# One decoder step on one core: the attention's work in another order, and the last stage shared out over four engines

## The reference, cut to what matters

```python
q = (xn @ wq).reshape(B, T, MEM_HEADS, MEM_HEAD_DIM)
s = jnp.einsum('bthd,bmhd->bhtm', q, k).astype(jnp.float32) * (MEM_HEAD_DIM ** -0.5)
p = jax.nn.softmax(s, axis=-1)
o = jnp.einsum('bhtm,bmhd->bthd', p, v).reshape(B, T, D_MODEL)
x = x + o @ wo
...
logits = (xt @ router_w).astype(jnp.float32)
top_v, top_i = lax.top_k(logits, TOP_K)
gates = jax.nn.softmax(top_v, axis=-1)
for e in range(N_EXPERTS):
    out = out + combine[:, e:e + 1] * swiglu(xt, wg[e], wu[e], wd[e])
...
return rmsnorm(x, P['final_norm'])
```

## Time and profile before

| what | value |
|---|---|
| median of 3 runs | 1127.97 us (1124.49 to 1130.51) |
| the profiled execution, whole | 1124.33 us |
| its span | 1122.5 us |
| PE busy | 1060.7 us (94%) |
| DVE busy, ACT busy, POOL busy | 781.1 us, 653.8 us, 21.4 us |
| shares of the chain that ended last | PE 74%, DVE 13%, ACT 6%, DMA 4% |

### The profile page before, as it was taken

One profiled execution on the slowest core, in us unless ns is written; L12 is line 12 of the kernel. 1 busy time (PEld: TensorE's weight loads), 2 busy tenths in 40 slices (PEclk: granted clock), 3 DMA queues, 4 the chain that ended last, 5 costly groups with the idle time before them and its releaser, 6 DMA issues.

```text
span 1122.5 us, 19890 instructions
## 1 busy us (share of the span) xinstructions
PE 1060.7 (94%) x7693; PEld 1003.4 (89%) x7693; DVE 781.1 (70%) x1080; ACT 653.8 (58%) x900; POOL 21.4 (2%) x40
## 2 busy tenths in 40 slices
PE   4999899999999998998999979999999999999994
PEld 4999897799999998998987869899999999999983
DVE  5597653575655556588553559798889888888973
ACT  5667433554433444576543457777767767776761
POOL 0001000000000000001010000000000000000000
PEclk8999999999999999999999989999999999999998
DMA  9454469946555555444469728898989898898951
GB/s 373 160 178 144 145 218 355 378 153 207 174 185 187 179 178 162 151 151 144 154 227 363 271 86 339 296 365 290 363 293 361 291 342 311 329 324 312 346 204 41
DMA packets 64275, 272.99 MB, mean 243 GB/s; under 512 B 7328, under 2 KB 7584, under 8 KB 63552
## 3 DMA queue, kind: packets, MB, share of 16 engines
q1 hardware_dynamic: 62352, 264.33, 66.1%
q0 software_dynamic: 1408, 7.12, 1.7%
q10 hardware_dynamic: 432, 0.38, 0.1%
HBM read 265.83 MB, written 5.98 MB: 242 GB/s over the span
## 4 chain that ended last, share of the span: by engine, by line
PE 74%; DVE 13%; ACT 6%; DMA 4%; issue 2%; SPq 1%; DVEq 0%; ACTq 0%
PE bank L645 11%; PE bank L648 11%; PE bank L650 11%; PE bank L649 11%; PE bank L646 11%; PE bank L647 11%; DMA ring<-dense 4%; DVE wl L1488 3%; ACT wh L1088 2%; DVE rstd L1482 2%; DVE sq L1499 1%; PE bank L672 1%; PE bank L765 1%; PE bank L937 1%; PE bank L938 1%
## 5 line engine op out<-in xcount | busy, mean ns | idle before, releaser
L1488 DVE TENSOR_TENSOR wl<-ring,wh 128x1024 fp32r<-128x1024 f32 x170 | 206.8, 1224 | 183.9 <-ACT wh L1088 182.4
L645 PE MATMUL bank<-xh,wh 128*128 128x264 f32 x928 | 271.2, 292 | 20.1 <-DVE xl L1504 17.1
L1088 ACT ACTIVATE wh<-ring 128x1024 fp32r<-128x1024 f32 x170 | 178.9, 1056 | 158.5 <-PE bank L647 121.3
L1757 DVE TENSOR_TENSOR wl<-ring,wh 128x1408 fp32r<-128x1408 f32 x144 | 232.5, 1623 | 52.8 <-ACT wh L1349 52.6
L646 PE MATMUL bank<-xl,wh 128*128 128x264 f32 x928 | 266.8, 288 | 0.0
L647 PE MATMUL bank<-xh,wl 128*128 128x264 f32 x928 | 266.3, 287 | 0.0
L1349 ACT ACTIVATE wh<-ring 128x1408 fp32r<-128x1408 f32 x141 | 194.7, 1381 | 52.5 <-PE bank L650 51.0
L645 PEld LDWEIGHTS bank<-xh,wh 128*128 128x128 f32 x928 | 178.1, 192 | 28.1 <-issue 23.0
L649 PE MATMUL bank<-wh,xl 128*128 128x352 f32 (+4 forms) x560 | 185.5, 331 | 0.0
L646 PEld LDWEIGHTS bank<-xl,wh 128*128 128x128 f32 x928 | 178.5, 192 | 0.0
L647 PEld LDWEIGHTS bank<-xh,wl 128*128 128x128 f32 x928 | 177.9, 192 | 0.0
(11 more groups left out here) (256 smaller groups left out, 1722.1 us busy)
## 6 DMA issues: line engine op xcount, KB each, us to landing
ring<-experts SPq DMA_DIRECT2D x192, 704.0 KB, 6.0
ring<-dense SPq DMA_DIRECT2D x234, 512.0 KB, 3.8
o_k<-kv POOLq DMA_DIRECT2D x2, 1024.0 KB, 4.3
o_v<-kv POOLq DMA_DIRECT2D x2, 1024.0 KB, 7.4
x<-xT SPq DMA_DIRECT2D x2, 528.0 KB, 5.0
o_y<-sq SPq DMA_DIRECT2D x4, 264.0 KB, 2.1
gatew<-gate_w POOLq DMA_DIRECT2D x2, 512.0 KB, 8.2
mem<-memT SPq DMA_DIRECT2D x1, 1024.0 KB, 13.4
```

What stands on the lines that cost most here:

```text
L645: mm(out, s_hi, m_hi, start=start, stop=False)
L1088: A(parts(k)[0], raw(u), ACT.Copy).then_inc(hi_ready, 1)
L1488: V.tensor_tensor(w_lo, raw(u), w_hi.bitcast(F32), ALU.subtract)\
L1757: V.tensor_tensor(w_lo, eraw(jj % ESLOTS), w_hi.bitcast(F32), ALU.subtract)\
```

## The change

**Attention.** PE takes the samples' scores of the last head directly behind those of the third, ahead of the prompt's scores; the samples' probabilities are turned between the two halves of the prompt's scores; the samples' values are spread between other work instead of standing in pairs. DVE and ACT treat the samples' softmax first. Both splitters run one unit less ahead in the queries (`4` for `5`). DVE copies the samples' result (`o8`) ahead of the first low part of `mo`, not behind it. POOL's stores of keys and values wait until the first bank of `mo` is full.

**Experts.** PE's wait for the rounded identity moves from ahead of the first gather to the place where the identity is used. PE, ACT and DVE load the count earlier: ACT and DVE ahead of the pass, PE in its last pair.

**The end.** The body that runs without `extra` is now the branch's first arm. PE scatters the first four chunks as soon as the first half of the last expert's result is split, and sums squares between later chunks. ACT squares each chunk when DVE has added it, multiplies `x` by `final_norm` itself, and has the square root's table loaded early. The last multiplication is split: DVE makes chunks 0, 1, 2, 4, 6 and POOL 3, 5, 7.

The number of ring slots is 10 before and after, although the change's title names it.

```diff
-                                if hp + hh + t + c == 1 and hp == 1:
+                                if hp + hh + t + c == 0:
                                     frees(i, ("kc", l, 15))
...
+                sample_scores(NH - 1)
                 prompt_scores(0)
-                sample_scores(NH - 1)
-                prompt_scores(1)
...
-                pe.wait_ge(p_ready, 5 * l + 3)
+                pe.wait_ge(p_ready, 5 * l + 1)
...
+                prompt_scores(1)
                 for h in (0, 1):
                     prompt_probs(h)
                 pe.wait_ge(pz_ready, l + 1)
                 sample_values(0)
-                sample_values(1)
                 for h in (2, 3):
                     prompt_probs(h)
+                sample_values(1)
...
                 for m in range(KC):
                     prompt_values(m)
-                sample_values(2)
+                    if m == 4:
+                        sample_values(2)
                 sample_values(3)
...
+                pe.wait_ge(ident_ready, 1)
                 for side in range(2):
...
+            def finish(ps):
+
+                num, before = ps.after, block_of(ps.last, "b")
+
+                def square_sum(m):
+                    b = take_bank(ps.final_sum) if m == 0 else bank(ps.final_sum)
+                    pe.wait_ge(fsq_ready, m + 1)
+                    i = mm(b[:, 0:T], ones[:, :], sq[:, m, :], start=(m == 0), stop=(m == KC - 1))
+                    if m == KC - 1:
+                        full(i, ps.final_sum)
+
+                wait_read(pe, *before("D0"))
+                for c in range(4):
+                    scatter_chunk(c, num)
+                wait_read(pe, *before("D1"))
+                for c in range(4, KC):
+                    scatter_chunk(c, num)
+                    square_sum(c - 4)
+                for m in range(4, KC):
+                    square_sum(m)
...
+                elif p == main.p0 + main.np - 1:
+                    fetch_count()
...
-            pe.wait_ge(ident_ready, 1)
...
+            with pe.If(counted[0] <= CAP):
+                finish(main)
+            with pe.Else():
+                scatter(main.after, block_of(main.last, "b"))
                 run_pass(extra)
-            with pe.Else():
-                pe.nop()
...
-                        S.upto(behind("mq", l, m, 5, start("mo", l)))
+                        S.upto(behind("mq", l, m, 4, start("mo", l)))
...
+                    if last and u == 0:
+                        A(small[:, 95:96], eps[:, 0:1], ACT.Sqrt)
...
+            def finish(ps):
+                for m in range(KC):
+                    wait_read(act, *ps.after(f"C{m}"))
+                    A(sq[:, m, :], x[:, m, :], ACT.Square).then_inc(fsq_ready, 1)
+
+                def final_gain(m):
+                    k = VEC_FINAL + m
+                    act.wait_ge(fsq_ready, m + 1)
+                    A(x[:, m, :], x[:, m, :], ACT.Copy, scale=vec[:, k:k + 1]).then_inc(xf_ready, 1)
+
+                for m in range(4):
+                    final_gain(m)
+                wait_full(act, ps.final_sum)
+                A(rms[:, 0, :], bank(ps.final_sum)[:, 0:T], ACT.Sqrt, bias=eps[:, 0:1], scale=1.0 / D).then_inc(frms_ready, 1)
+                for m in range(4, KC):
+                    final_gain(m)
+
             act.wait_ge(route_ready, 1)
             count = act.value_load(need[0:1, 0:1], min_val=0, max_val=T)
+            run_pass(main)
...
-                S.upto(start("mo", l) + 1, 0)
                 n = tiles[("pvs", l)]
                 wait_full(dve, n)
                 read(V.tensor_copy(o8, bank(n)[:, 0:HD]), n)
+                S.upto(start("mo", l) + 1, 0)
...
+            def finish():
+
+                dve.wait_ge(frms_ready, 1)
+                V.reciprocal(rstd[:, 0, :], rms[:, 0, :]).then_inc(frstd_ready, 1)
+                dve.wait_ge(frstd_ready, 1)
+                for m in (0, 1, 2, 4, 6):
+                    dve.wait_ge(xf_ready, m + 1)
+                    V.tensor_tensor(xn[:, m, :], x[:, m, :], rstd[:, 0, :], ALU.mult).then_inc(y_ready, 1)
...
+                wait_full(pool, tiles[("mo", l, 0)])
                 pool.dma_start(o_k[l], kT).then_inc(kv_written, 16)
...
+            pool.wait_ge(frstd_ready, 1)
+            for m in (3, 5, 7):
+                pool.wait_ge(xf_ready, m + 1)
+                G.tensor_tensor(xn[:, m, :], x[:, m, :], rstd[:, 0, :], ALU.mult).then_inc(y_pool_ready, 1)
```

More of the change, by code:

```diff
@@ L155, in bank_plan @@
         out += [("scs", l)]
-        out += [("sc", l, t, hp) for hp in range(2) for t in range(2)]
+        out += [("sc", l, t, 0) for t in range(2)]
         out += [("pts", l)]
+        out += [("sc", l, t, 1) for t in range(2)]
         out += [("pt", l, h) for h in range(NH)]
@@ L207, in __init__ @@
             self.end = self.tail + len(TAIL)
+            self.final_sum = self.end
         def first(self, kind):
@@ L1042, in run_pass @@
                 pair(p1, ps.last, ps.earlier(p1), last=True)
-                scatter(ps.after, block_of(ps.last, "b"))
             for t in range(3):
@@ L1047, in _, with fetch_count @@
                     wait_read(pe, tiles[("tk", l, t, hp)])
-            pe.wait_ge(ident_ready, 1)
+            counted = []
+            def fetch_count():
+                pe.wait_ge(route_ready, 1)
+                counted.append(pe.value_load(need[0:1, 0:1], min_val=0, max_val=T))
             run_pass(main)
-            pe.wait_ge(route_ready, 1)
-            count = pe.value_load(need[0:1, 0:1], min_val=0, max_val=T)
-            with pe.If(count > CAP):
+            with pe.If(counted[0] <= CAP):
+                finish(main)
+            with pe.Else():
+                scatter(main.after, block_of(main.last, "b"))
                 run_pass(extra)
-            with pe.Else():
-                pe.nop()
-            for m in range(KC):
-                pe.wait_ge(fsq_ready, m + 1)
-                i = mm(psum[0][:, 0:T], ones[:, :], sq[:, m, :], start=(m == 0), stop=(m == KC - 1))
-            i.then_inc(fsum_ready, 1)
+                finish(extra)
         @block.scalar
@@ L1239, in _ @@
                     if m % 2:
-                        S.upto(behind("mq", l, m, 5, start("mo", l)))
+                        S.upto(behind("mq", l, m, 4, start("mo", l)))
+                n = tiles[("scs", l)]
+                act.wait_ge(max_ready, 5 * l + 1)
+                read(A(prs, bank(n)[:, 0:NM], ACT.Exp, bias=nmx[:, 8:9], scale=HD ** -0.5, accum_out=sm[:, 8:9]), n)
                 for hp in range(2):
@@ L1254, in _ @@
                                 i.then_inc(exp_done, 1)
-                    if hp == 0:
-                        n = tiles[("scs", l)]
-                        act.wait_ge(max_ready, 5 * l + 3)
-                        read(A(prs, bank(n)[:, 0:NM], ACT.Exp, bias=nmx[:, 8:9], scale=HD ** -0.5, accum_out=sm[:, 8:9]), n)
                 for h in range(NH):
@@ L1427, in run_pass @@
                 pair(p1, ps.last, last=True)
-            run_pass(main)
+            def finish(ps):
[12 more added lines that the diff above has]
+                    final_gain(m)
             act.wait_ge(route_ready, 1)
             count = act.value_load(need[0:1, 0:1], min_val=0, max_val=T)
-            with act.If(count > CAP):
+            run_pass(main)
+            with act.If(count <= CAP):
+                finish(main)
+            with act.Else():
                 run_pass(extra)
-            with act.Else():
-                act.nop()
-            act.wait_ge(x_final, 1)
-            for m in range(KC):
-                A(sq[:, m, :], x[:, m, :], ACT.Square).then_inc(fsq_ready, 1)
-            act.wait_ge(fsum_ready, 1)
-            A(rms[:, 0, :], psum[0][:, 0:T], ACT.Sqrt, bias=eps[:, 0:1], scale=1.0 / D).then_inc(frms_ready, 1)
+                finish(extra)
         @block.vector
@@ L1653, in _ @@
                         signal(qz_ready)
-                        S.upto(behind("mq", l, c, 5, start("mo", l)))
+                        S.upto(behind("mq", l, c, 4, start("mo", l)))
                 if l % 2:
@@ L1691, in _ @@
                 signal(p_ready)
-                for t in range(2):
-                    top(t, 1)
+                top(1, 0)
+                normalize(0, 0)
                 n = tiles[("pts", l)]
@@ L1707, in _ @@
                 signal(pz_ready)
+                normalize(1, 0)
+                for t in range(2):
+                    top(t, 1)
                 for t in range(2):
@@ L1943, in _ @@
                 elow(0, j)
+            dve.wait_ge(route_ready, 1)
+            count = dve.value_load(need[0:1, 0:1], min_val=0, max_val=T)
             run_pass(main)
-            count = dve.value_load(need[0:1, 0:1], min_val=0, max_val=T)
-            with dve.If(count > CAP):
+            with dve.If(count <= CAP):
+                finish()
+            with dve.Else():
                 run_pass(extra)
-            with dve.Else():
-                dve.nop()
```

(8 more changed lines are left out.)

38 lines of the change are left out of this document (21 added, 17 removed).

## The result

| | median of 7 runs | range |
|---|---|---|
| before | 1126.14 us | 1124.23 to 1130.51 |
| changed | 1118.82 us | 1118.16 to 1122.65 |

The ratio is 0.9943, with a 95% interval of 0.9926 to 0.9959: 6.4 us faster (4.6 to 8.3); the medians differ by 7.3. Forecast were 10.8 us and a median of 1117.2. That the median came within 1.6 us of its forecast owes something to chance: the 10.8 were taken from a median of 1127.97 over three runs, which over seven runs is 1126.14. The profiled execution has a span of 1116.3 us, 6.2 less than before, with PE busy for 1061.6 us as before (1060.7): the same work, and less standing still.

What follows compares the result with a forecast made beforehand. PE, busy for 94% of the span, was taken as the bound, with most to gain where stages take turns at the end. Attention 2.3 + experts' start 0.9 + end 7.6 = 10.8 us off 1127.97: 1117.2, range 1110 to 1122.5.

Steps and rivals of the forecast that it cites:

- The order of the last scores: Both attentions: third and fourth heads' scores need `kc` units sooner, a new wait of 0.4 us in each layer.
- unit 0 of `mo` would land sooner: Output projection's first load: lands about 0.5 us sooner, its slot freed by earlier products of PE.
- The parts behind the query copies: Both attentions: waits before the second head's samples' scores go, 0.91 us in the first layer, 0.56 in the second.
- the wait ahead of the values: Both attentions: PE's wait before the samples' values goes, 0.46 us in each layer, as the softmax has more cover.
- The tail: From the values' end to the first product of `mo`: 2.7 us, before 3.13 and 2.97 in the two layers.
- Late stores: POOL's stores of keys and values, issued some 4 us into `mo`: cost nothing, with slack of 20 and 5 us.
- The half clock of the first `mo`: Start of first `mo`: 1.7 us lost to half clock may be spared or recur elsewhere; bounds widened 1.7 either way.
- The experts' start: First gather: PE starts 1.7 us sooner, at about 663, partly at half speed; gain 0.9 us (0 to 1.7).
- The end: From PE's last expert product to the span's end: reciprocal 8.0 us earlier, 0.4 given back, net gain 7.6 us.
- the tail behind the reciprocal: Reciprocal's end to span's end: 6.2 us instead of 5.86, from multiplications 3.7, landing 2.1 and the rest 0.43.
- a jump at the arm's end: End of the branch over `extra`: the jump stays and may outlast the stores by 0.4 us.
- the third rival: Attention: new waits reach 0.91 per layer, loads set `mo`, half clock in second layer; total 7.6 to 8.5; chance 0.08.

Runs made afterwards that it cites:

- Experiment 3: The changed kernel with the last head's samples' scores back between the halves of the prompt's scores, and the softmax order with it: 1113.88 us, ratio 0.9886.
- experiment 9: The changed kernel, its scores' order kept, with a head's samples' scores between the halves of the next head's query products: 1116.33 us, ratio 0.9908.
- experiment 8: The kernel of Experiment 3 with both splitters five units ahead in the queries again: 1117.23 us, ratio 0.9919.
- experiment 5: The kernel of Experiment 3 with POOL's stores of keys and values early again: 1113.79 us, ratio 0.9888.
- Experiment 1: The kernel before with only the changed end, count loads and identity wait, attention as before: 1119.1 us, ratio 0.9942.
- 11: The kernel of Experiment 3 with PE's wait for the rounded identity ahead of the first gather again: 1114.03 us, ratio 0.9878.
- experiment 4: The changed kernel with all eight last multiplications on DVE, none on POOL: 1120.21 us, ratio 0.9944.
- experiments 2: The kernel before with the change's attention alone, end and experts' start as before: 1128.96 us, ratio 1.0015.
- 12: The kernel before with one edit, both splitters four units ahead in the queries instead of five: 1122.17 us, ratio 0.9966.

## Why the prediction was right in direction and too high by 4 us

**The order of the last scores was the step that failed.** The prediction allowed for a wait there: "the third and fourth heads' scores now run without prompt's scores between them and need `kc` units sooner", priced at 0.4, with a bound of 0.91, the longest wait in its rows. It measured 1.84 and 1.88. A wait was priced by other waits, where it should have come from a landing: the load's landing time and the time at which PE would ask for the unit were both in the trace of before, and give 1.5. Experiment 3 shows its worth (4.2 us in the spans of both attentions, 5 by the medians), experiment 9 that the late unit is its cause. With it fell the sentence that unit 0 of `mo` would land sooner: it landed at 206.43, before at 206.23, since a PE that waits frees its slots later (without that wait, in experiment 3, it landed at 204.45).

**The parts behind the query copies** were right: 0.91 and 0.56 are gone, and experiment 8 gives them a price of its own. The second term that failed is the wait ahead of the values: its 0.46 was to go, but became one of 0.36 ahead of the probabilities, and with the scores' order back 0.45 are left. Of 0.9 us in two layers 0.2 came. **The tail** to `mo` was forecast at 2.7 us and is 210.90 - (209.06 - 0.72) = 2.56 in the first layer, 2.56 in the second. The size held, though not for the reason given: unit 0 came no sooner, but the values ended 1 us later (208.34, before 207.31).

**Late stores** cost nothing, as said, and bring nothing (experiment 5). The half clock of the first `mo` went, and one came at the second: both of the cases that the bound of 1.7 allowed for, with little effect on the sum. Experiment 1, whose attention is that of before, has one at each `mo`.

**The experts' start**, forecast 0.9: PE's wait there is 1.3 shorter (4.64 for 5.96), forecast 1.7, and the gather came at 665.47, not at about 663. The traces of experiments 3 and 11 show some half of the 1.3 given back behind the gather, as the prediction feared, which leaves 0.6; their runs can't tell it from nothing.

**The end**, forecast 7.6 and measured 6.2. Up to the reciprocal the working held: 10.4 us behind the last expert product, forecast 10.2. No stall stands behind the compares; PE's first scatter product follows the expert's last without a gap. The term that was too small is the tail behind the reciprocal: 7.45, forecast 6.2. Its multiplications held: 3.44 us, forecast 3.7, with 2.60 / 3 = 0.87 for a product on POOL beside DVE (forecast 0.64 alone). The Trainium skill, page "SBUF — State Buffer", section "Who interferes with whom", had them exclude each other, and the trace agrees: 0.96 for a product of DVE beside one of POOL's, 2.84 / 8 = 0.36 for each of eight without. The records don't show the turns themselves: DVE's and POOL's products overlap, and DVE's are longer than alone (POOL's alone were not measured). What was missed is the stores: their last one is issued at 1112.45, 0.44 us behind the third, and lands at 1115.59, 3.1 later; the sum took 2.1 from a row in which stores stand 0.81 apart. Another 0.3 stands behind the landing, 0.7 to the end of the span instead of 0.4. The prediction had named a jump at the arm's end that may cost 0.4, but experiment 4 has the same jump and 0.4 behind its landing, so the cause of the 0.3 is open.

So the third rival came closest, with a wait twice as long as it allowed. In the profiled execution the attentions and the end give -2.1 + 6.2 = 4.1, where 2.3 + 7.6 = 9.9 were forecast. All the rest, the experts' start included, gives 2.1, forecast 0.9. At least 1.3 us of it lie where a stretch at half clock happens to be missing, so it is in part luck that the whole was missed by no more than 4.6. One slip in the prediction's chances: its cases over 5.6 add up to 0.93, not 0.91.

## What to carry to other kernels

When PE is moved ahead, ask for each unit of data when it lands, not only whether PE waited for it before: where the DMA engines run without a gap, the landing stays and the saved time comes back as a wait. Work that needs no load, as the prompt's scores here, belongs in front of what needs the latest one. And a split over two engines is to be priced with both working side by side: here it made the multiplications 0.6 us longer. What stands behind it needs a price of its own, as the last store's landing took 1 us more than the row from which it was forecast.

## What the runs showed of the hardware

- Products on DVE and POOL, both with two inputs in SBUF, hinder each other: five on DVE need 3.44 us beside three on POOL, eight need 2.84 alone. This is what turns would give; the records can't tell turns from sharing.
- Stores of 264 KB land 2.1 us behind their issue when they stand 0.81 apart (before, experiments 2 and 12), and the last one 2.9 to 3.5 when it is issued 0.43 to 0.48 behind another (all other traces). In experiment 4 stores that stand 0.69 apart take 2.75 too; why is not shown.
- Loads of 512 KB that are queued while the DMA engines move 416 GB/s land one every 1.3 us (177.64, 178.91, 180.20 and 181.47 in the changed kernel). The time from issue to landing, 5.6 to 7.9 us for the last four `kc` units, is there a place in the queue.
- Stretches of 3.4 us and more at half clock come at other places in each profiled execution, also in a stage that was left as it was (a granted clock of 0.50 from 626.2 to 629.6 in experiment 1, where before has none at that place), so that one execution's stage differs by 1.7 us for this alone.
